# Multiplying twenty-four modulation blocks of the first layer on TensorE inside the attention units

## The reference, cut to what matters

```
for l in range(DEPTH):
    mod = jax.nn.silu(c) @ w_ada[l] + b_ada[l]
    sh1, sc1, g1, sh2, sc2, g2 = jnp.split(mod[:, None, :], 6, axis=-1)
    h = rms_norm(x, norm_g[l, 0]) * (1.0 + sc1) + sh1
    ...                       # three mixers: two attentions (a, c) and a scan (b)
    mix = jnp.concatenate([o_a, o_b, o_c], axis=-1) @ w_out[l]
    x = x + g1 * mix
    h = rms_norm(x, norm_g[l, 1]) * (1.0 + sc2) + sh2
    x = x + g2 * conv_ffn(h, w_up[l], conv_w[l], conv_b[l], w_down[l])
```

## Time and profile before

| | us |
|---|---|
| median of 3 runs | 2473.94 |
| lowest, highest | 2468.49, 2475.46 |
| the profiled execution, its own time | 2471.28 |
| its span, first to last instruction | 2469.5 |
| TensorE busy | 2407.2 (97%) |
| VectorE busy | 1612.8 (65%) |
| ScalarE busy | 847.6 (34%) |

### The profile page before, as it was taken

One profiled execution on the slowest core, in us unless ns is written; L12 is line 12 of the kernel. 1 busy time (PEld: TensorE's weight loads), 2 busy tenths in 40 slices (PEclk: granted clock), 3 DMA queues, 4 the chain that ended last, 5 costly groups with the idle time before them and its releaser, 6 DMA issues.

```text
span 2469.5 us, 46042 instructions
## 1 busy us (share of the span) xinstructions
PE 2407.2 (97%) x17350; PEld 2234.2 (90%) x17350; DVE 1612.8 (65%) x3756; ACT 847.6 (34%) x2183; POOL 298.9 (12%) x386
## 2 busy tenths in 40 slices
PE   7989999999999999999999999999899999999998
PEld 6868889878888987999999999989599999999998
DVE  6886665574666273795888883325639958888634
ACT  2542120443110113223665540022622246655300
POOL 1030110010110001010111121100401101111110
PEclk9999999999999999999999999999999999999999
DMA  8447888314889562699999999954038989999997
GB/s 321 158 166 280 305 291 331 129 59 147 312 302 360 198 245 78 224 413 347 401 408 402 407 405 414 394 193 162 1 129 316 414 325 409 407 396 413 406 413 294
DMA packets 171489, 727.06 MB, mean 294 GB/s; under 512 B 19152, under 2 KB 19664, under 8 KB 146384
## 3 DMA queue, kind: packets, MB, share of 16 engines
q1 hardware_dynamic: 142992, 521.76, 56.4%
q0 software_dynamic: 27648, 201.34, 20.1%
q10 hardware_dynamic: 704, 2.10, 0.4%
HBM read 721.97 MB, written 1.05 MB: 293 GB/s over the span
## 4 chain that ended last, share of the span: by engine, by line
PE 87%; DVE 6%; DMA 3%; ACT 2%; issue 2%; POOL 0%; SPq 0%; DVEq 0%; ACTq 0%
PE banks L749 36%; PE lev L1152 23%; PE banks L1098 21%; DMA ring<-in_peer_u 2%; PE lev L749 2%; PE banks L1079 1%; PE lev L1079 1%; PE banks L865 1%; PE banks L921 1%; DMA extra<-in_ada 1%; DVE arena L1965 1%; DVE arena L2031 0%; ACT arena L1423 0%; DVE arena L1991 0%; DVE arena L1894 0%
## 5 line engine op out<-in xcount | busy, mean ns | idle before, releaser
L749 PE MATMUL banks<-hT,ring 128*128 128x256 f32 (+1 forms) x2832 | 584.5, 367 | 4.8 <-ACT hT L1332 3.2
L1098 PE MATMUL banks<-hT,ring 128*128 128x160 f32 x4096 | 579.4, 301 | 3.6 <-DMA ring<-in_peer_u 3.3
L749 PEld LDWEIGHTS banks<-hT,ring 128*128 128x128 f32 x2832 | 513.1, 190 | 72.5 <-ACT hT L1332 5.0
L1152 PE MATMUL lev<-arena,ring 128*128 x4096 | 576.8, 301 | 0.0
L1098 PEld LDWEIGHTS banks<-hT,ring 128*128 128x128 f32 x4096 | 559.2, 190 | 5.3 <-DMA ring<-in_peer_u 1.9
L1152 PEld LDWEIGHTS lev<-arena,ring 128*128 128x128 f32 x4096 | 559.0, 190 | 0.2
L1781 POOL DMA_INDIRECT arena<-in_peer_rows,keysb x192 | 184.9, 963 | 1131.5 <-DVE consts L2192 675.0
L749 PE MATMUL banks<-arena,ring 128*128 128x256 f32 (+2 forms) x1648 | 284.9, 334 | 0.7 <-DVE arena L2049 0.7
L749 PEld LDWEIGHTS banks<-arena,ring 128*128 128x128 f32 x1648 | 259.1, 192 | 25.4 <-DVE arena L2049 1.1
L2239 DVE SCALAR_TENSOR_TENSOR extra<-consts,chT 128x192 bf16<-128x192 f32 x640 | 223.8, 409 | 17.8 <-ACT arena L1471 17.6
L2204 DVE CUSTOM_DVE_ANT_0 arena<-arena 128x1024 f32<-128x1024 f32 x64 | 78.2, 1222 | 165.2 <-DMA arena<-in_peer_rows,keysb 165.1
(11 more groups left out here) (286 smaller groups left out, 2284.3 us busy)
## 6 DMA issues: line engine op xcount, KB each, us to landing
ring<-in_peer_u SPq DMA_DIRECT2D x256, 512.0 KB
ring<-in_peer_v SPq DMA_DIRECT2D x256, 512.0 KB
ring<-in_stream_first SPq DMA_DIRECT2D x188, 512.0 KB
arena<-in_ada SPq DMA_DIRECT2D x104, 512.0 KB, 5.4
extra<-in_ada SPq DMA_DIRECT2D x88, 512.0 KB, 5.3
ring<-in_stream_nsa SPq DMA_DIRECT2D x45, 512.0 KB
ring<-in_stream_fox SPq DMA_DIRECT2D x41, 512.0 KB
arena<-in_peer_rows,keysb POOLq DMA_INDIRECT x192
```

The source lines that it names most:

```text
L749: ins = nc.tensor.matmul(o, lhsT, rhs, start=start, stop=stop, **kw)
L1098: ins = nc.tensor.matmul(banks[k // 2 % 4][:, (k % 2) * ND:(k % 2 + 1) * ND], ring[:, u % RING, c], hT[:, c, NS:T], start=c == 0, stop=c = ...
L1152: ins = nc.tensor.matmul(lev[c // 4][:, (c % 4) * T + NS:(c % 4 + 1) * T], ring[:, u % RING, c], a[:, bass.ds(g, 1), k], start=False, stop ...
```

## The change

The twenty-four blocks 16 to 39 of the first layer (`GATE_ROWS`) are laid out anew by the host, as eight 128 x 128 pieces with the input channel on the partition, so that a piece can be the stationary operand of a product. silu(c) is also held with the channel on the partition (`ccol`, 8 chunks of 2 equal columns, made by one more ScalarE instruction near the start). In the first layer's attention, job j multiplies blocks 16 + 2j and 17 + 2j (`gate_products`): each is eight f32 products of 128 x 128 by 128 x 2, summed into two free columns of the unit's output bank. They stand where `keep_warm` stood; the seven zero products of each of the twelve units are gone. VectorE adds the bias to the one column of each block ahead of copying the unit's output (two additions of 128 x 1 in each unit), and reads none of the 24 blocks. The loads of blocks 20 to 39 wait for TensorE's products (`gate_rows`); their places in SP's order become 10 behind unit 25 and 10 behind unit 26.

```diff
+GATE_ROWS = range(2 * DC, 5 * DC)
...
+    put("ccol", np.repeat(ch(g["c"][0]), 2, 1))
...
+    for n in GATE_ROWS:
+        out["ada"][0, n] = g["w_ada"][0][:, n * P:(n + 1) * P].reshape(DC, P, P).transpose(1, 0, 2).reshape(P, D)
...
-        ADA_LOADS = {RING + 6: 4, U_IN + 5: 10, U_IN + 7: 4, U_IN + 8: 2, U_IN + 9: 2, U_IN + 10: 2}
-        ADA_UNITS, ADA_OUT = [[0] * 4 + [1] * 6 + [2] * 2, [0] * NATT], [(5, 5, 4, 0), (0, 0, 0, 0)]
+        ADA_LOADS = {RING + 6: 4, U_IN + 5: 10, U_IN + 6: 10}
+        ADA_UNITS, ADA_OUT = [[0] * NATT, [0] * NATT], [(0, 0, 0, 0), (0, 0, 0, 0)]
+        GATE_JOBS = [{j: (16 + 2 * j, 17 + 2 * j) for j in range(NATT)}, {}]
...
-                    if n >= 16 + ADA_RING:
-                        sp.wait_ge(sem("ada_used"), n - ADA_RING + 1)
+                    if n >= GATE_ROWS.stop + ADA_RING:
+                        sp.wait_ge(sem("ada_used"), n - ADA_RING + 1 - len(GATE_ROWS))
+                    elif n >= 16 + ADA_RING:
+                        sp.wait_ge(sem("gate_rows"), n - ADA_RING - 16 + 1)
...
+            def gate_products(b, rows):
+
+                for i, n in enumerate(rows):
+                    if n == GATE_ROWS[0]:
+                        pe.wait_ge(sem("c_col"), 1)
+                    pe.wait_ge(sem(f"ada_in{n % ADA_RING}"), 16 * ((n - 16) // ADA_RING + 1))
+                    for c in range(DC):
+                        mm(b[:, T + 2 * i:T + 2 * i + 2], ada_slot(n)[:, c * P:(c + 1) * P], ccol[:, c], c == 0, c == DC - 1,
+                           sem("gate_rows") if c == DC - 1 else None)
...
-                            keep_warm(ob[:, 0:T], warm_values)
+                            if jobs - 1 in gates:
+                                gate_products(ob, gates[jobs - 1])
+                            else:
+                                keep_warm(ob[:, 0:T], warm_values)
...
+            A(ccol, ccol, ACT.Silu).then_inc(sem("c_col"), 1)
...
+                    if ada_n[0] == GATE_ROWS[0]:
+                        ada_n[0] += len(GATE_ROWS)
...
+                        for i, r in enumerate(gates.get(jobs - 1, ())):
+                            seq(V.tensor_tensor(mod[:, 0, r // DC, r % DC:r % DC + 1], bank_of(*j)[:, T + 2 * i:T + 2 * i + 1],
+                                                col("bada", 0, r), ALU.add))
...
-                if l == 0:
-                    mods(0, 2, 3)
```

More of the change, by code:

```diff
@@ L75, in columns @@
                     ("nq", 1), ("nkc_lo", 1), ("nkc_hi", 1), ("nks", 1), ("nkw", 1),
-                    ("bgate", 48), ("pos", 2 * CMP_LEN)):
+                    ("bgate", 48), ("pos", 2 * CMP_LEN), ("ccol", 2 * DC)):
         at[name] = n
@@ L623, in build @@
         ADA_FOX = (9, 18, 23, 29)
-        ADA_LOADS = {RING + 6: 4, U_IN + 5: 10, U_IN + 7: 4, U_IN + 8: 2, U_IN + 9: 2, U_IN + 10: 2}
-        ADA_UNITS, ADA_OUT = [[0] * 4 + [1] * 6 + [2] * 2, [0] * NATT], [(5, 5, 4, 0), (0, 0, 0, 0)]
+        ADA_LOADS = {RING + 6: 4, U_IN + 5: 10, U_IN + 6: 10}
+        ADA_UNITS, ADA_OUT = [[0] * NATT, [0] * NATT], [(0, 0, 0, 0), (0, 0, 0, 0)]
+        GATE_JOBS = [{j: (16 + 2 * j, 17 + 2 * j) for j in range(NATT)}, {}]
+        ccol = col("ccol", None, 0, 2 * DC).rearrange("p (c a) -> p c a", a=2)
         EARLY = 2 * DEPTH * ADA
@@ L890, in level, with attention @@
                            signal=sem("lev_filled") if h == 3 and t == 1 else None)
-            def attention(name, us, u0, beside={}, warm={}, warm_values=0):
+            def attention(name, us, u0, beside={}, warm={}, warm_values=0, gates={}):
                 n, jobs = len(us), 0
@@ L991, in _ @@
                           {1: lambda: pe.wait_ge(sem("lev_freed"), NLEV * (l + 1)), 2: outputs_B, NATT: lambda: stat("statB", l, 1, "sqB", l + 1),
-                           6: lambda: pe.wait_ge(sem("qkC"), l + 1)}, *WARM_ATT[l])
+                           6: lambda: pe.wait_ge(sem("qkC"), l + 1)}, *WARM_ATT[l], GATE_JOBS[l])
                 mixed = {c: [freed("att", l, 2 * (c if c < 3 else c - 2) + t) for t in range(TT)] for c in (0, 1, 2, 5, 6, 7)}
@@ L1817, in mods @@
                 m = mod[:, l, a:b]
-                seq(V.tensor_tensor(m, m, col("bada", l, a * DC, (b - a) * DC).rearrange("p (a c) -> p a c", c=DC), ALU.add))
+                if l or a * DC not in GATE_ROWS:
+                    seq(V.tensor_tensor(m, m, col("bada", l, a * DC, (b - a) * DC).rearrange("p (a c) -> p a c", c=DC), ALU.add))
                 for w in range(2):
@@ L1875, in residual, with attention @@
                     scale(1, c, "h_scaled")
-            def attention(name, us, u0, projections=None, beside={}):
+            def attention(name, us, u0, projections=None, beside={}, gates={}):
                 n, jobs = len(us), 0
@@ L2051, in _ @@
                 attention(("att", l), units_of(l), l * NATT, ADA_UNITS[l],
-                          {0: lambda: None if l == 0 else roots_C(3), 1: lambda: roots_C(0), 2: lambda: roots_C(1), 3: lambda: roots_C(2), 4: norm_C, NATT + 2: lambda: roots_B(0), NATT + 3: lambda: roots_B(1)})
+                          {0: lambda: None if l == 0 else roots_C(3), 1: lambda: roots_C(0), 2: lambda: roots_C(1), 3: lambda: roots_C(2), 4: norm_C, NATT + 2: lambda: roots_B(0), NATT + 3: lambda: roots_B(1)}, GATE_JOBS[l])
                 norm_B()
-                if l == 0:
-                    mods(0, 2, 3)
                 residual(2 * l + 1, ("out", l), l, 2, ADA_OUT[l], None if l else lambda: mods(0, 3, 5))
```

## The result

| | before | after |
|---|---|---|
| median of 4 runs, us | 2472.94 | 2530.31 |
| lowest, highest | 2468.49, 2475.46 | 2525.1, 2534.35 |
| the profiled execution | 2471.28 | 2534.35 |
| its span | 2469.5 | 2532.6 |
| the attention stretch, to the output projection | 34.9 | 103.0 |

The ratio is 1.0236, with a 95% interval of 1.0219 to 1.0253: 57.4 us more.

The account below looks back on a forecast made before the run. TensorE was taken to bound attention, its clock falling for part of it. The terms 48.5 (attention) + 1.7 (cold start) + 0.2 (ScalarE instruction) - 3.7 (output projection) gave +46.7 us, forecast 2520, range 2490 to 2535.

Parts of the forecast that it names:

- What bounds: First layer's attention: TensorE alone sets the pace, 60.5 us of work against the 34.9 us there were.
- The price of a record: New products in attention: 0.112 us for each of 384 records at full clock, 43.0 us in all.
- the faster rival: Weight loads hidden in attention, 0.029 us a record; VectorE's waits go too: -9.7 us, 2464; chance 0.05.
- the half-way one: A record in attention costs 0.07 us, the middle of two ends: +6.0 us, 2480; chance 0.05.
- The sum at the full clock: Attention: 17.5 us of needed work plus 43.0 of products, 60.5 us, ending 25.6 us later.
- the clock stays: Rival: 2.4 GHz holds through attention if weight loads count as work: +22.1 us, 2496; chance 0.31.
- Two-column products with their weight loads don't hold the clock: Attention: loads don't count as work, so the clock falls after a unit's products; attention ends 48.5 us later.
- The share of time at half clock: s, in attention: taken as 0.55, range 0.4 to 0.75; the stretch T becomes 83.4 us.
- A half-clock record "doubles": Attention's two-column records: 0.112 us at full clock becomes 0.22 at half clock.
- s = 1: Rival: clock down through the whole attention, T = 121 us, +84 us in all, 2558; chance 0.06.
- the formula: Attention's length T from s, the share at half clock: T x (1 - s/2) = 60.5 us.
- The output projection: First layer: 3.7 us comes back without VectorE's 14 reads; 1.7 us lost if it starts at half clock.

Follow-up runs that it names:

- the wide kernels: After with each new product streaming 128 equal columns instead of 2, 2491.1 us; and the same with four of each block's eight products, 2475.1 us.
- the wide kernel: After with each new product streaming 128 equal columns instead of 2, same 384 records and weights; 2491.1 us, ratio 1.0073.
- short reads: Before with VectorE's 14 output-projection block reads cut to 16 of 1024 columns, 2469.2 us; with the 10 in attention cut too, 2462.86 us.

## Why the prediction was right, and where it was off

It forecast slower, 2520 with a range of 2490 to 2535; the time is 2530.3, inside, 10 us above the forecast. The mechanism was the one forecast; one term of the sum, the share of time at the low clock, was sized too small. By its steps:

- **What bounds.** TensorE alone, as said: no idle time in 103 us.
- **The price of a record**, 0.112 us at the full clock, the row of 30 columns. Right: 32 records in 3.63 us, and 0.104 to 0.107 as the slope of the wide kernels. The low bound of 0.029, from bf16 zero weights, was far off, and with it the faster rival and the half-way one.
- **The sum at the full clock.** 60.5 us of work predicted; the kernel with wide products, which holds the clock, took 61.4. The rival "the clock stays" was 2496; that kernel ran at 2491.
- **Two-column products with their weight loads don't hold the clock.** Right, and it was the choice that mattered most: 39 us lie between the two kernels that differ in width alone. "TensorE: Matmul & The Clock Gate" of the Trainium skill, in its section on LDWEIGHTS, prices a load by its columns alone; the trace doesn't agree at the low clock, 6.95 us for 32 loads against 3.65.
- **The share of time at half clock is the term that was mis-sized.** I took 0.55, on the step that the clock "returns after its dense part". It returned after two of the eleven dense parts between the jobs' products. The share was (103 - 11) / 103 = 0.89, outside the 0.4 to 0.75 that I gave it. The stretch took 103.0 us where 83.4 was forecast: 19.6 us short. The 0.55 doesn't follow from the step itself either. The half-clock part of a unit, 3.4 us, is shorter than the 3.58 of products at the full clock, not longer; over the stretch the step gives 43.0 + 2 x 17.5 = 78.0 us, a share of 0.45 and about 2515.
- **A half-clock record "doubles".** Nearly: 6.83 for 3.63, a factor of 1.88, and the dense part of a unit takes 3.1 us for 1.72. So even s = 1 would have given about 113 us, not 121. This is an estimate from the rows: the 103.0, with 3.2, 3.1 and 2.9 us more for the three groups that ran at the full rate and under 1 us for what ran fast beside them. The miss in s therefore cost less than the formula says. The rise of the stretch over its 34.9 us is 68.1 against 48.5.
- **The output projection**, -3.7 with +1.7 for its cold start. Right: the stage took 38.2 us, and the two parts stand apart in the runs: 36.4 with the clock up (231.70 - 195.28 in the wide kernel, and the same with the short reads), and 26.32 against 24.56 at its start.
- **The rest.** Attention began 0.9 us earlier than before, not 0.2 later (133.42 against 134.32). That is no effect of the change: with the same code ahead of it as in after, it began at 133.87 in the wide kernel and at 134.40 with the zero products back, and with that of before at 133.59 without them. So 68.1 - 2.2 - 0.9 = 65.0 us at the first up-projection group behind the stage (274.59 against 209.65); the later 2258 us gave 1.9 of it back, which no run explains. No load was late, as forecast, though the reach of a load was overstated: by the prediction's own unit of 5.3 us, two units less one block's 1.8 us are 8.8 us, not over 10.
- **The sum of the errors.** The stretch was 19.6 us too short. The start (1.1), the output projection (0.2) and the later stages (1.9) make up 3.2 of it; the profiled execution of after is 4.0 above its median and that of before 1.7 below its own. 19.6 - 3.2 - 5.7 = 10.7, the miss of the median's rise (57.4 against 46.7). That the time lies inside the range is in part luck: s lies outside the span that the range was built on, and by the forecast's own formula with the measured share, T = 60.5 / (1 - 0.445) = 109 us, the time would have come out at 2546, outside it. The formula's doubling was too much, and that made up for a part of s.

VectorE's relief was judged rightly. The prediction bounded TensorE's waits in attention at 6.2 us and let the products cover them; with short reads alone the stretch is 5.7 us shorter. In after the waits are gone as well; they lie under the products.

## What to carry to other kernels

Where a product's weights are used once, look for its price in a row with weights of the same size and type, and count records, not columns: here 0.11 us each, with two columns, with 30 and with 128. Where the columns cost nothing beside the load, stream more of them, even copies of one: here two columns were followed by the low clock, which slowed everything around them, and 128 were not. Before moving work off an engine, cut it short in place to see the most that this can give: here 10.3 us, against 43 us on the receiving engine. And where two engines read one ring of slots, look for a circle through the loads.

## What the hardware showed that was not expected

- TensorE without idle time is no sign of a high clock: 103 us of it stood at a mean of 0.55 of full speed, while 33.1 us with 13.3 of them idle, in waits of 2.3 us at most, held 1.00.
- The time of a weight load depends on the clock: 32 f32 loads of 128x128 took 3.65 us at 2.4 GHz and 6.95 at 1.2.
- 128 columns of f32 are nearly free beside an f32 load of 128 x 128: 3.74 us for 32 records, against 3.63 with two columns.
- Seven zero products a unit, 0.93 us, moved the mean clock from 0.55 to 0.64 and no further, and the full clock came mostly behind them: in eight of the twelve narrow groups, against three in after. Which parts of a unit bring it back, and why two late groups of after had it at 199 and 206 us, stays open.
